# Last feed-forward part: second layer by rows of tokens, sums kept in PSUM, gate multiplied into the weights, norm with tokens on partitions

## The reference, cut to what matters

```python
# h: 256 x 1024; w1: 1024 x 4096; w2: 4096 x 1024; g2: one gate per feature
h = x * (1 + sc2) + sh2
a = maximum(h @ w1, 0)
x = layer_norm(4 ** 0.25 * x + g2 * ((a * a) @ w2), ln2_g, ln2_b)
```

## Time and profile before

| what | value |
|---|---|
| runs, median (lowest to highest) | 1951.69 us (1950.99 to 1953.96) |
| the profiled execution's own time | 1957.06 us |
| its span, first to last instruction | 1955.3 us |
| mean granted TensorE clock | 0.950 of full |
| PE busy | 1749.1 us, 9480 matmuls |
| DVE busy | 964.8 us, 1761 instructions |
| ACT busy | 644.1 us, 1105 instructions |
| chain that ended last | PE 65%, DVE 15%, DMA 10%, ACT 7% |

### The profile page before, as it was taken

How to read it: one execution, slowest core, us unless ns; L and a number is a source line. 1 busy time by engine, 2 the same in 40 slices (tenths; PEclk the granted TensorE clock), 3 DMA queues, 4 the chain that set the end, 5 groups by cost and what they waited for, 6 DMA issues and landing times.

```text
span 1955.3 us, 23433 instructions
## 1 busy us (share of the span) xinstructions
PE 1749.1 (89%) x9480; PEld 1210.7 (62%) x9480; DVE 964.8 (49%) x1761; ACT 644.1 (33%) x1105; POOL 94.8 (5%) x136
## 2 busy tenths in 40 slices
PE   6998867998998679989989979999999798889997
PEld 5654633443676224447445658888887574679996
DVE  5673400002444000144577465887676846666665
ACT  2154121122232111132266445222232525654443
POOL 0790000000000000000000000000000100000000
PEclk8989989999999889999989989999999898989999
DMA  9978499999858999982200112445453121024530
GB/s 391 378 297 325 185 405 421 421 421 421 324 201 326 399 403 418 420 350 87 86 1 1 44 44 93 187 175 212 173 214 151 65 89 41 4 103 176 186 137 22
DMA packets 61863, 430.10 MB, mean 220 GB/s; under 512 B 6576, under 2 KB 9776, under 8 KB 9904
## 3 DMA queue, kind: packets, MB, share of 16 engines
q1 hardware_dynamic: 61744, 428.48, 54.9%
HBM read 427.40 MB, written 1.05 MB: 219 GB/s over the span
## 4 chain that ended last, share of the span: by engine, by line
PE 65%; DVE 15%; DMA 10%; ACT 7%; issue 2%; SPq 1%; DVEq 0%; ACTq 0%
PE bank L292 14%; PE bank L1100 11%; PE bank L296 10%; PE bank L298 9%; PE bank L297 9%; DMA ring<-in_ws_dram 7%; DMA work<-in_ws_dram 3%; DVE ring_halves L2421 2%; PE bank L331 2%; ACT work_halves L2415 2%; PE bank L2094 2%; PE bank L2071 2%; DVE work L438 1%; PE bank L2445 1%; DVE work L553 1%
## 5 line engine op out<-in xcount | busy, mean ns | idle before, releaser
L296 PE MATMUL bank<-work_halves 128*128 128x512 f32 (+1 forms) x1344 | 472.4, 351 | 29.0 <-DVE HH_halves L2713 15.1
L298 PE MATMUL bank<-work_halves,ring_halves 128*128 128x512 f32 (+1 forms) x1344 | 461.1, 343 | 0.0
L296 PEld LDWEIGHTS bank<-work_halves 128*128 128x128 f32 x1344 | 258.5, 192 | 66.4 <-DVE HH_halves L2713 16.2
L297 PE MATMUL bank<-HH_halves,work_halves 128*128 128x512 f32 (+1 forms) x832 | 289.3, 348 | 0.0
L1100 PE MATMUL bank<-ring,work 128*32 128x512 f32 (+2 forms) x896 | 257.7, 660 | 21.5 <-DMA work<-in_ws_dram 11.2
L298 PEld LDWEIGHTS bank<-work_halves,ring_halves 128*128 128x128 f32 x1344 | 258.4, 192 | 28.7
L1100 PE MATMUL bank<-work 128*32 128x512 f32 (+2 forms) x640 | 222.0, 640 | 35.8 <-DMA ring<-in_ws_dram 34.1
L2421 DVE TENSOR_TENSOR ring_halves<-ring,work_halves 128x2048 fp32r<-128x2048 f32 x72 | 164.7, 2287 | 51.0 <-ACT work_halves L2415 51.0
L297 PEld LDWEIGHTS bank<-HH_halves,work_halves 128*128 128x128 f32 x832 | 161.6, 194 | 20.5 <-issue 2.2
L297 PE MATMUL bank<-work_halves 128*128 128x512 f32 (+1 forms) x512 | 172.0, 336 | 0.0
L1378 DVE TENSOR_TENSOR work<-work,bank 128x512 f32<-128x512 f32 x14 | 9.6, 688 | 298.8 <-PE bank L1100 298.8
(11 more groups left out here) (339 smaller groups left out, 2291.0 us busy)
## 6 DMA issues: line engine op xcount, KB each, us to landing
ring<-in_ws_dram SPq DMA_DIRECT2D x287, 1024.0 KB, 10.3
work<-in_ws_dram SPq DMA_DIRECT2D x117, 1024.0 KB, 18.2
con<-in_con_dram SPq DMA_DIRECT2D x1, 1177.0 KB, 27.3
XX<-in_xT_dram SPq DMA_DIRECT2D x1, 1024.0 KB, 10.0
XX<-in_cT_dram SPq DMA_DIRECT2D x1, 1024.0 KB, 20.2
out_dram<-XX SPq DMA_DIRECT2D x2, 512.0 KB, 3.1
par<-in_par_dram SPq DMA_DIRECT2D x1, 338.0 KB, 2.9
con<-in_con_dram SPq DMA_DIRECT2D x1, 128.0 KB, 2.8
```

The lines of the kernel that those rows point to most:

```text
L296: pe.matmul(out, l[0], r[0], start=start, stop=False)
L297: pe.matmul(out, l[0], r[1], start=False, stop=False)
L298: return pe.matmul(out, l[1], r[0], start=False, stop=stop)
```

## The change

Only in the last block. The second layer is turned round: 128 tokens are the stationary operand and 512 output features of the weights move (`pe_rows`), so the output has tokens on partitions, in four banks (two halves of the tokens t, two halves of the features j) that hold their sums over all eight hidden parts. The residual is added by matmuls with the identity (`pe_residual`). The gate now lies along the free dimension; it is spread over the partitions by a matmul of ones with a diagonal (`pe_g2`), kept in `self.g2`, and multiplied into each second-layer tile on DVE ahead of the split (`dve_scale(i + 3)`, behind `split_dve(i + 2)`); `split_act` waits for it. The first layer's results rotate over the other four banks. The norm takes moments along the free dimension (bn_stats), PE transposes the result back, DVE and ACT apply gain and bias on the way out of PSUM, and three transfers write the output.

```diff
--- before.py
+++ after.py
@@ -2379,6 +2379,13 @@
+        if self.last:
+            self.g2, self.diag = work[:, 13312:14336], XX[:, 0:4, 256:512]
+            self.acc = [[bank[2 + 2 * t + j] for j in range(2)] for t in range(2)]
+            self.y = [work[:, 14336 + 1024 * t:15360 + 1024 * t] for t in range(2)]
+            self.moments = [small[:, 176 + 12 * t:188 + 12 * t] for t in range(2)]
+            self.mv = [small[:, 200 + 2 * t:202 + 2 * t] for t in range(2)]
+            self.root, self.rt, self.nb = [[small[:, 204 + 2 * i + t:205 + 2 * i + t] for t in range(2)] for i in range(3)]
@@ -2395,16 +2402,36 @@
+        self.rf = Rota([0, 1, 6, 7], ro) if self.last else ro
+        if self.last:
+            for i in range(4):
+                ro.put(2 + i, "sum", i)
...
-                for m in range(2 if name == "fc1" else 4):
-                    ro.take(name, f, 2 * j + m if name == "fc1" else 4 * j + m)
+                if name == "fc1" or not self.last:
+                    for m in range(2 if name == "fc1" else 4):
+                        self.rf.take(name, f, 2 * j + m if name == "fc1" else 4 * j + m)
...
-        ro.take("var", 1)
+        if self.last:
+            for t in range(2):
+                for q in range(4):
+                    self.rf.take("back", t, q)
+        else:
+            ro.take("var", 1)
+    def scaled(self, i):
+        return self.last and i < len(self.w) and self.w[i][0] == "fc2"
+    def dve_scale(self, dve, i):
+        if self.scaled(i):
+            st, w, j = self.st, k8(ring_of(self.w[i]), 512), self.w[i][3]
+            st.wait_ge(dve, "g2 at hand", j)
+            loaded(dve, self.w[i])
+            dve.tensor_tensor(w, w, self.g2[:, 512 * j:512 * j + 512].unsqueeze(1).broadcast_to([P, 4, 512]), MUL).then_inc(st.dve("scaled", i), 1)
...
     def split_act(self, act, i):
@@ -2412,6 +2439,8 @@
+            if self.scaled(i):
+                st.wait_ge(act, "scaled", i)
...
     def split_dve(self, dve, i):
@@ -2465,6 +2494,8 @@
+        if self.last:
+            self.pe_g2(pe)
@@ -2475,19 +2506,78 @@
+                elif not self.last:
+                    self.pe_fc2(pe, f, j, i)
+                elif f < 7:
+                    for t in range(2):
+                        self.pe_rows(pe, f, t, j, i)
+                    if (f, j) == (0, 1):
+                        self.pe_residual(pe)
+                elif j == 0:
+                    self.pe_rows(pe, 7, 0, 0, i)
...
-                    self.pe_fc2(pe, f, j, i)
+                    self.pe_rows(pe, 7, 0, 1, i)
+                    self.pe_rows(pe, 7, 1, 0, i - 1)
+                    self.pe_back(pe, 0)
+                    self.pe_rows(pe, 7, 1, 1, i)
+                    self.pe_back(pe, 1)
...
-        self.pe_sum(pe, 1, 6)
-        self.pe_sum(pe, 1, 7)
-        self.pe_norm(pe, 1)
+        if not self.last:
+            self.pe_sum(pe, 1, 6)
+            self.pe_sum(pe, 1, 7)
+            self.pe_norm(pe, 1)
+    def pe_g2(self, pe):
+        st = self.st
+        st.wait_ge(pe, "diag")
+        st.wait_ge(pe, "mu", 0)
+        for j in range(2):
+            mms(pe, k8(bank[7 - j][:, :], 256), [(ones, self.diag[:, 2 * j:2 * j + 2, :])]).then_inc(st.pe("g2", j), 1)
+    def pe_rows(self, pe, f, t, j, i):
+        st = self.st
+        fh, fl = [k8(r_(a), 512) for a in self.Fs[f % 2]]
+        wh, wl = self.weight(i, 512)
+        c, b = slice(P * t, P * t + P), self.acc[t][j]
+        if f == 0:
+            bank_of(pe, st, self.ro, "sum", 2 * t + j)
+        for k in range(4):
+            st.wait_ge(pe, "fl", f, k)
+            pe.matmul(b[:, :], fh[:, k, c], wh[:, k, :], start=f == k == 0, stop=False, skip_group_check=True)
+            pe.matmul(b[:, :], fh[:, k, c], wl[:, k, :], start=False, stop=False, skip_group_check=True)
+            m = pe.matmul(b[:, :], fl[:, k, c], wh[:, k, :], start=False, stop=f == 7 and k == 3, skip_group_check=True)
+        m.then_inc(st.pe("rows", f, t, j), 1)
+        if t == 1:
+            st.at["used", self.w[i]] = st.at["rows", f, t, j]
+            if j == 1:
+                st.at["fc2", f, 7] = st.at["rows", f, t, j]
+    def pe_residual(self, pe):
+        st = self.st
+        for o in range(8):
+            st.wait_ge(pe, "a", o)
+            for t in range(2):
+                c = slice(P * (o % 4), P * (o % 4) + P)
+                pe.matmul(self.acc[t][o // 4][:, c], XX[:, o, P * t:P * t + P], ident, start=False, stop=False, skip_group_check=True)
+    def pe_back(self, pe, t):
+        st = self.st
+        for q in range(4):
+            b = bank_of(pe, st, self.rf, "back", t, q)
+            st.wait_ge(pe, "y", t, q // 2)
+            for o in (2 * q, 2 * q + 1):
+                m = pe.transpose(b[:, P * (o % 2):P * (o % 2) + P], self.y[t][:, P * o:P * o + P], ident)
+            m.then_inc(st.pe("back", t, q), 1)
...
     def pe_fc1(self, pe, f, js, i):
...
+        if self.last and f == 0:
+            for j in range(2):
+                st.wait_ge(pe, "g2 at hand", j)
...
@@ -2543,6 +2633,10 @@
+        if self.last:
+            for j in range(2):
+                st.wait_ge(act, "g2", j)
+                act.activation(self.g2[:, 512 * j:512 * j + 512], bank[7 - j][:, :], ACT.Copy).then_inc(st.act("g2 at hand", j), 1)
@@ -2565,13 +2659,34 @@
+        if self.last:
+            self.act_last(act, 0)
+            self.act_out(act, 0)
+            self.act_last(act, 1)
+            self.act_out(act, 1)
+            return
...
+    def act_last(self, act, t):
+        st = self.st
+        st.wait_ge(act, "moments", t)
+        act.activation(self.root[t], self.mv[t][:, 1:2], ACT.Sqrt, bias=EPS).then_inc(st.act("root", t), 1)
+        st.wait_ge(act, "shift", t)
+        act.activation(self.y[t][:, 512:1024], self.acc[t][1][:, :], ACT.Identity, scale=self.rt[t], bias=self.nb[t]).then_inc(st.act("y", t, 1), 1)
+    def act_out(self, act, t):
+        st = self.st
+        for q in (1, 3):
+            st.wait_ge(act, "back", t, q)
+            for o in (2 * q, 2 * q + 1):
+                m = act.activation(X1[:, o, P * t:P * t + P], bank[self.rf.of["back", t, q][0]][:, P * (o % 2):P * (o % 2) + P], ACT.Identity,
+                                   scale=par_("l2g1", o), bias=par_("l2b1", o))
+            m.then_inc(st.act("evicted", ("back", t, q)), 1)
...
     def act_relu(self, act, f, m):
...
@@ -2627,6 +2742,11 @@
     def dve(self, dve):
...
+        if self.last:
+            self.M.wait_mod(dve, 2)
+            gain = mod[:, 40:48, 0].rearrange("p (a b) -> p a b", b=2).unsqueeze(3).broadcast_to([P, 4, 2, P])
+            dve.tensor_tensor(self.diag.rearrange("p a (b n) -> p a b n", b=2), ident.unsqueeze(1).unsqueeze(1).broadcast_to([P, 4, 2, P]),
+                              gain, MUL).then_inc(st.dve("diag"), 1)
@@ -2656,7 +2776,7 @@
-                else:
+                elif not self.last:
@@ -2664,9 +2784,20 @@
+                    self.dve_scale(dve, i + 3)
...
+        if self.last:
+            self.dve_stats(dve, 0, 0)
+            self.dve_stats(dve, 0, 1)
+            self.dve_last(dve, 0)
+            self.dve_stats(dve, 1, 0)
+            self.dve_out(dve, 0)
+            self.dve_stats(dve, 1, 1)
+            self.dve_last(dve, 1)
+            self.dve_out(dve, 1)
+            return
@@ -2678,12 +2809,32 @@
...
+    def dve_stats(self, dve, t, j):
+        st = self.st
+        st.wait_ge(dve, "rows", 7, t, j)
+        dve.bn_stats(self.moments[t][:, 6 * j:6 * j + 6], self.acc[t][j][:, :]).then_inc(st.dve("half moments", t, j), 1)
+    def dve_last(self, dve, t):
+        st, mv = self.st, self.mv[t]
+        for j in range(2):
+            st.wait_ge(dve, "half moments", t, j)
+        dve.bn_aggr(mv, self.moments[t]).then_inc(st.dve("moments", t), 1)
+        st.wait_ge(dve, "root", t)
+        dve.reciprocal(self.rt[t], self.root[t]).then_inc(st.dve("rt", t), 1)
+        st.wait_ge(dve, "rt", t)
+        dve.tensor_scalar(self.nb[t], mv[:, 0:1], self.rt[t], -1.0, MUL, MUL).then_inc(st.dve("shift", t), 1)
+        dve.tensor_scalar(self.y[t][:, 0:512], self.acc[t][0][:, :], mv[:, 0:1], self.rt[t], SUB, MUL).then_inc(st.dve("y", t, 0), 1)
+    def dve_out(self, dve, t):
+        st = self.st
+        for q in (0, 2):
+            st.wait_ge(dve, "back", t, q)
+            for o in (2 * q, 2 * q + 1):
+                m = dve.tensor_scalar(X1[:, o, P * t:P * t + P], bank[self.rf.of["back", t, q][0]][:, P * (o % 2):P * (o % 2) + P],
+                                      par_("l2g1", o), par_("l2b1", o), MUL, ADD)
+            m.then_inc(st.dve("evicted", ("back", t, q)), 1)
...
     def dve_square(self, dve, f, m):
@@ -2776,11 +2927,11 @@
-    for a in (0, 4):
-        for k in range(a, a + 4):
-            ffn1.st.wait_ge(sp, "x", k)
-        sp.dma_start(d["out"][:, a:a + 4, :], XX[:, a:a + 4, 0:256]).then_inc(s_out, 16)
-    sp.wait_ge(s_out, 32)
+    for t, a, b in ((0, 0, 4), (1, 0, 2), (1, 2, 4)):
+        for q in range(a, b):
```

(30 more changed lines are left out.)

## The result

The changed kernel takes 1976.0 us (median of four runs, 1974.0 to 1978.2) against 1952.1 us for the kernel before: the ratio is 1.012, with a 95% interval of 1.0105 to 1.0134, so it is slower by 23.9 us. The prediction was 1975.0 us. Its profiled execution took 1975.4 us.

The account below looks back on a forecast made before the run. The prediction took the DVE and ACT wait chain, not PE, as the bound. 0.8 + 16.3 + 5.7 - 8.5 = +14.3 us, plus 9 for the clock, is +23.3 on 1951.7: 1975 us, range 1962 to 1981.

Parts of the forecast that it names:

- What bounds: Last feed-forward rounds: the DVE and ACT wait chain holds the 23.45 us round; PE's own need is 23.04.
- Columns: Second layer: 512-column matmuls cut a tile from 5.76 to 5.44 us, 0.32 less; only one tile a round counts.
- The multiplication: Gate multiplication on DVE: 2.21 us each, one in each round's chain; round 25.34 us, +1.89, PE pausing about 2.9.
- First rounds: Last part's start: +2.2 before the first round, +1.2 in it, 9.4 over five more, residual 3.5; together 16.3 us.
- Last tiles: Last square to last second-layer matmul: multiplications alternate with ACT's rounding and DVE's remainders, 30.8 to 36.5 us, +5.7.
- Norm and front: After the last matmul 8.7 us instead of 17.2, -8.5; gate diagonal ahead of the attention's remainders, +0.8.
- Clock: PE's granted clock drops to 1.2 GHz after six of eight new pauses: 9 us, bounds 0 to 12.
- The price of the multiplications: Of the +14.3 us without the clock, 22.8 come from multiplications on the chain at 2.2 us each.
- break-even: Price per multiplication at which the change would neither gain nor lose: near 0.8 us.
- The clock holds: Rival: same chain, but PE's pauses stay short enough to cost no clock; 1966 us, chance 0.25.
- Half the price: Rival: part of each multiplication fits DVE's waits for ACT; +2.9 without the clock, about 1957 us, chance 0.08.
- Faster: Rival: multiplications fit DVE's idle time, off the chain, and PE is the limit; -9, 1943 us, chance 0.05.

Follow-up runs that it names:

- e3: Changed kernel with the multiplication of each round's second second-layer tile moved behind the other one, a round ahead; last two tiles as changed: 1956.0 us, ratio 1.0007.
- e6: Changed kernel with weight tiles' work first in each step (as e4) and each multiplication a step earlier, last in DVE's step: 1938.9 us, ratio 0.9922.
- e9: e6 with each of the 384 second-layer matmuls of 512 columns cut into two of 256: 1943.1 us, ratio 0.9939.
- e7: e6 with the residual matmuls ahead of PE's wait for tile 7 and the gate diagonal behind DVE's first residual addition: 1937.3 us, ratio 0.9918.
- e2: Changed kernel with 20 idle 256-column matmuls on PE ahead of its wait for each round's second second-layer tile, but the last: 1969.0 us, ratio 1.0076.
- e1: Changed kernel without the 16 gate multiplications and ACT's wait for them (gate left out of the result): 1944.6 us, ratio 0.9955.
- e8: Changed kernel with each multiplication cut to the first half of its tile, 128 x 1024, in the same place: 1957.3 us, ratio 1.0017.
- e4: Changed kernel with the weight tiles' rounding, remainder and multiplication ahead of the step's ReLU and squares in the last block: 1952.1 us, ratio 0.9992.
- e5: Kernel before with weight tiles' rounding and remainder ahead of the step's ReLU, squares and additions in the last block: 1953.6 us, ratio 0.9994.
- e10: Changed kernel with only the last two second-layer tiles' multiplications moved ahead by three steps: 1972.1 us, ratio 1.0092.

## Why the prediction was right

*What bounds.* That the chain over DVE and ACT holds the round, and not PE with its 99%, was right: e3 and e6 keep DVE's work, and by moving it they lose its cost, e3 in the rounds, e6 in the whole part.

*Columns.* 0.31 us a tile (e9) against 0.32. As forecast the chain hid most of it; in e6 and e7, where PE is the limit, it pays.

*The multiplication.* 2.29 us and 2.21 to the next start, as taken from the remainder's row; the rounds without a drop are 25.36 us against 25.34 forecast, and e2's 25.37. The pause of PE was 2.6 us and not 2.9, since PE's busy time in such a round is 22.72 us and not 22.40. Without a pause the same matmuls take 22.42 (e6); around a pause a matmul's record runs longer (0.39 and 0.50 us) than the 0.227 counted for it.

*First rounds.* 30.53 us, +6.4, against 1.2 + 3.5 and a drop of 1.5. The residual's matmuls take 3.49 us (1784.87 to 1788.36), forecast 3.5.

*Last tiles.* The alternation of DVE and ACT came to the tenth: b1's remainder ends 13.4 us after the square, tile 35's 26.45 after it (1952.30 + 2.29), forecast 13.4 and 26.4. The end part takes 37.55 us where the forecast has 36.5 without the clock: 1.1 more, for the drop behind tile 35's pause. The pause ahead of tile 35 was 3.06, not 3.6. The two clock drops of this part are not two full prices: the one in b1 (behind the pause ahead of 1941.56) fell where PE would have waited for DVE's remainders anyway.

*Norm and front.* 7.9 us for 8.7, and +0.6 for +0.8. The moments take 0.70 us for 512 columns, as the reduction's row said. The last write, on ACT, ends at 1968.95 + 1.51 = 1970.46:

```profile
1968.95 1.51 ACT L2687 ACTIVATE XX<-bank,par 128x128 f32<-128x128 f32 x4 [0.72 <-PE bank L2571]
```

From there to the end are 3.2 us, where 3.8 had been carried over from before; that is most of the 0.8, and why it is shorter no run shows.

*Clock.* The least certain term: six drops forecast, 9 us. Up to the norm PE ran at 1.2 GHz after seven of the eight pauses of 2.6 us and more. A round with a drop is 27.0 - 25.36 = 1.63 us longer, and there are four of them: 6.5. The first round holds another, 6.4 - 1.2 - 3.5 = 1.7, and the two of the end part cost 1.1 together. That is 9.2 us or so. The size is right, but not the count: six full prices were forecast, and there were five, and two drops that cost less than one. That six was taken, between none and eight, had a weak reason (one row), and so the hit is in part luck. Luck is also that 1976.0 agrees with 1975 to 1 us: the common code ahead of the change differs by 4 us between two executions.

*The price of the multiplications.* The prediction's 22.8 us, on which its break-even rests, is not derived there. The runs bear it out: from e1's trace to the change's are 32.2 us, and without the clock's 9.2 some 23.

*The rivals.* "The clock holds" did not come true; e2, with PE kept busy, shows what it would have been in the rounds: +13.7 measured, +14.3 forecast without the clock. "Half the price" falls with the rows of the change, where all 2.21 us of a multiplication pass on; its sum was +2.9, and e8, with half the instruction, gives +3.1. "Faster" is a matter of place, which e6 shows; the change didn't put it there. Its break-even, near 0.8 us a multiplication, agrees with e1 and e8: without a multiplication -10.7, at 1.2 us +3.1, with zero near 0.9 on the line between them.

## What to carry to other kernels

An in-order engine that is idle for a third of the time can still hold the kernel: what counts for an added instruction is whether the engine waits where it stands, or whether somebody waits behind it. Put precomputation of weights at the place of the queue where nobody waits, a round ahead of its use if need be (e6), and look at the first and the last tiles by themselves, since a steady round that has become shorter may only push its debt to them (e4, e5). Where PE is made to pause by 2 to 3 us in each round, add to the pause the price of the clock, here 1.6 us on a pause of 2.6, where the clock's drop lies on the path.

## What was not expected of the hardware

After pauses of 2.61 to 2.64 us the granted clock mostly fell to 1.2 GHz, for some 3.4 us, but not after the one ahead of 1916.19, which is as long; e10 has the same picture, with the exception at the same round. Before, 2.24 us had cost nothing and 2.41 a drop; but 2.35 us ahead of 1769.33 in the change and 2.47 in e8 cost none. After the pauses of 1.5 to 1.6 us of e8 no round showed one. So among pauses from 2.41 to 2.64 us the length alone does not decide. What else does stays open; no run here tells it. The price goes up steeply between these pauses and e8's: with 1.1 us more in each pause the kernel goes from e8's +3.1 us to +23.9, and some 9 of these 21 us are the clock's.
